# Last stage of a streaming encoder step: the order of the frame products and the expert rows on TensorE

## The chip, the cores and the metric

The kernel runs on one core of a Trainium2 chip. The metric is device time in microseconds (us) for one execution of the whole step, from inputs in device memory to outputs in device memory. The profile calls the engines PE (TensorE), DVE (VectorE), ACT (ScalarE), POOL (GpSimd) and SP (SyncE, which here only issues DMAs); SPq and POOLq are what the profile lists of their instruction queues.

## The reference, cut to what matters

The step is one encoder layer over 2048 prompt frames and 32 sample frames: a projection, two kinds of attention, an output mixer with a LayerNorm, a mixture of experts, and a last LayerNorm. Only the last line concerns us. Each frame has chosen two experts, with two gates, and the layer ends in

```python
x = layer_norm(ALPHA * x + grouped_moe(x, ...), ln2_g, ln2_b)   # ALPHA = 2 ** 0.25
# grouped_moe: for each frame, gate0 * expert0(x) + gate1 * expert1(x)
```

So for a frame with row `h` and the two expert rows `y0` and `y1`, the output is `LN(ALPHA*h + g0*y0 + g1*y1) * ln2_g + ln2_b` over 1024 columns in float32.

## The kernel before, in words

The kernel is written engine by engine, in stages; every engine's instructions stand in the order in which the code issues them, and semaphores tie the engines together. The change is in the last stage, `combine` (from L2971). By then the frames lie in device memory (`scratch_h`), and all expert rows, not yet gated, in `scratch_ypad`.

The stage works on 17 tiles of 128 frames (the last has 32), in four slots: tile `t` uses slot `t % 4` of every buffer, and each slot has its own pair of PSUM banks, `Z[s]`, so that all eight banks are used.

- **SP** loads the frames of tile `t` into `z_h` (L3013; from tile 4 on it first waits until tile `t-4` is summed) and stores finished tiles (L3020). Its order is: loads 0 and 1, the two weight rows, loads 2 and 3, then for each `t`: load `t+4`, store `t`. A store waits for POOL's and DVE's last work on its tile, and load `t+5` stands behind store `t`.
- **POOL** gathers the two expert rows of each frame with two indirect DMAs per tile (L3045), four tiles ahead, and adds the bias to the second half of the columns (L3057).
- **ACT** makes two diagonal matrices of gates per tile, `z_diag` (L3088), takes the square root for the norm (L3106), and applies the norm from PSUM into `z_z` (L3096).
- **PE** sums a tile by matmuls: `ALPHA` times the identity (`z_scaled`) by the frames, which I call the frame product (L3070), and for each of the two experts the diagonal matrix by the gathered rows, the expert rows (L3075). A tile has two halves of 512 columns, so it takes two frame matmuls and four expert matmuls. The frame matmul begins an accumulation, and waits for the frame's load and, from tile 4 on, for the norm of tile `t-4`, which reads the same banks last. The expert matmuls wait for gates and gathered rows. After the last matmul of a tile the semaphore step `sum` is given.
- **DVE** waits for `sum`, takes the statistics from PSUM (L3130 to L3133), multiplies tile `t-1` by the gain and adds half of its bias (L3123, L3124), and then ends tile `t`'s reciprocal and shift (L3137, L3138), for which ACT's norm of tile `t` waits.

Of the kernel before, what the change touches and what calls it, by code (L numbers as in the profile page):

```python
# [19 lines left out]
TILES = NT + 1  # L20
# [2950 lines left out]
def combine(nc, io, keep):  # L2971

    with ExitStack() as ctx:  # L2973
        def sb(name, shape, dt=F32):
            return ctx.enter_context(nc.sbuf_tensor(name, shape, dt))

        def sem(name):
            return ctx.enter_context(nc.semaphore(name))

        SLOTS = 4
# [5 lines left out]
        diag = sb("z_diag", [P, SLOTS, 2, P])  # L2987
# [5 lines left out]
        y_loaded = [sem(f"z_y_loaded{s}") for s in range(SLOTS)]  # L2993
# [3 lines left out]
        diags = Steps(sem("z_diag_steps"), ["diag"])  # L2997
# [4 lines left out]
        HALF = D // 2  # L3002

        def turn(t):
            return t % SLOTS, t // SLOTS

        @block.sync
        def _(sp):
            def load(t):
                s, _ = turn(t)  # L3010
                if t >= SLOTS:
                    sp.wait_ge(*pe.after("sum", t - SLOTS))
                sp.dma_start(h[:, s, :], io["h"][t * P:(t + 1) * P, :]).then_inc(h_loaded[s], 16)  # L3013

            def store(t):
                s, _ = turn(t)
                sp.wait_ge(*pool.after("out", t))
                sp.wait_ge(*done.after("out", t))
                dst = io["y_sample"][0] if t == NT else io["y_prompt"][0, t * P:(t + 1) * P, :]
                sp.dma_start(dst, z[0:NEW if t == NT else P, s, :]).then_inc(stored[s], 16)  # L3020

            load(0)
            load(1)
            sp.dma_start(gain[:, :], io["ln2_g"].broadcast_to([P, D])).then_inc(weights_loaded, 16)
            sp.dma_start(offset[:, :], io["ln2_b"].broadcast_to([P, D])).then_inc(weights_loaded, 16)
            load(2)
            load(3)
            for t in range(TILES):
                if t + SLOTS < TILES:
                    load(t + SLOTS)  # L3030
                store(t)
            for s in range(SLOTS):
                sp.wait_ge(stored[s], 16 * len(range(s, TILES, SLOTS)))
# [25 lines left out]
        @block.tensor  # L3059
        def _(eng):  # L3060
            pe.begin(eng)
            eng.wait_ge(scaled_made, 1)
            for t in range(TILES):
                s, n = turn(t)
                eng.wait_ge(h_loaded[s], 16 * (n + 1))
                if t >= SLOTS:
                    eng.wait_ge(*act.after("norm", t - SLOTS))
                for half in (0, 1):
                    at = slice(half * HALF, (half + 1) * HALF)
                    eng.matmul(Z[s][:, at], scaled[:, :], h[:, s, at], start=True, stop=False)  # L3070
                    if half == 0:
                        eng.wait_ge(*diags.after("diag", t))
                        eng.wait_ge(y_loaded[s], 32 * (n + 1))
                    for i in (0, 1):
                        mm = eng.matmul(Z[s][:, at], diag[:, s, i, :], y[:, s, i, at], start=False, stop=(i == 1))  # L3075
                mm.then_inc(*pe.done("sum"))

        @block.scalar
        def _(eng):
# [63 lines left out]
def build(nc, io):  # L3143

    with ExitStack() as ctx:
# [9 lines left out]
        with ExitStack() as inner:  # L3155
# [28 lines left out]
            mix(nc, io, keep)  # L3184
            experts(nc, io, keep)
        combine(nc, io, keep)

# [37 lines left out]
```

## Time and profile before

| what | value |
|---|---|
| time before, median of 3 runs | 3857.66 us (3852.83 to 3857.68) |
| the profiled execution's own time | 3855.51 us |
| its span, first to last instruction | 3853.7 us |
| first instruction of the last stage (a DMA issue) | 3740.1 us after the span's start |
| first matmul of the stage, first expert row | 3743.80 us, 3753.20 us |
| first and last statistics on DVE | 3759.28 us, 3841.61 us |
| PE busy over the whole span | 3629.9 us (94%) |
| mean granted TensorE clock over the span | 0.97 |

The last stage is the last 113 us or so of the span. All times of day below are us after the span's start. In the rows of the timeline a bracket at the end says how long the engine had been idle, and what released it. The float32 matmuls of this stage show as two records each, so a matmul of the program is "x2" in a row; a matmul's record lasts longer than the distance to the next, as they are pipelined, and the chain of waits gives the distance.

### The profile page before, as it was taken

The numbers are of one execution on the slowest core, as the hardware profiler recorded it, in microseconds if no ns is written. First come the engines' busy times: TensorE is split into PE (matmuls) and PEld (weight loads), VectorE is DVE, ScalarE is ACT, GpSimd is POOL, SyncE is SP. The second block draws the span as 40 slices with busy tenths as digits, with TensorE's granted clock in tenths as the row PEclk, the third lists the DMA queues.
The fourth block names the chain that finished last, engine by engine and source line by source line (L and its number), as shares of the span: only waits on it lengthen the run. The fifth ranks groups of instructions, "written<-read, shape, count | busy, mean of one in ns | idle before, by whom it ended". The sixth has DMA issues, their size and how long they took to land. (4 is left out here: it accounts for less than half of the span.)

```text
span 3853.7 us, 77787 instructions
## 1 busy us (share of the span) xinstructions
PE 3629.9 (94%) x30285; PEld 2174.0 (56%) x30286; DVE 1628.0 (42%) x3569; ACT 954.7 (25%) x1730; POOL 236.8 (6%) x350
## 2 busy tenths in 40 slices
PE   7999997999999999988999989978999999999988
PEld 4444446888888888874555655543333333333333
DVE  1221224666666666666777645560111111111108
ACT  2222221323232323225555521110000000000003
POOL 0000001000000000001111000000000000000005
PEclk9999998999999999988999999988999999999999
DMA  5122212000000000002211152226566567744427
GB/s 218 61 74 74 74 59 61 10 10 19 10 19 10 19 11 19 11 9 81 59 56 56 45 189 92 99 83 269 216 265 255 198 267 283 299 152 159 158 113 305
DMA packets 145519, 430.34 MB, mean 112 GB/s; under 512 B 30696, under 2 KB 73840, under 8 KB 132976
## 3 DMA queue, kind: packets, MB, share of 16 engines
q1 hardware_dynamic: 126736, 359.27, 25.1%
q0 software_dynamic: 11616, 42.21, 3.1%
q10 hardware_dynamic: 6912, 25.17, 1.7%
q8 instruction: 195, 3.19, 0.3%
q14 instruction: 60, 0.49, 0.0%
HBM read 750.99 MB, written 78.27 MB: 215 GB/s over the span
## 5 line engine op out<-in xcount | busy, mean ns | idle before, releaser
L297 PE MATMUL fp<-f_w,f_xT 128*128 128x512 f32 (+1 forms) x1360 | 533.8, 547 | 9.8 <-DMA f_w<-in_w_in 9.5
L716 PE MATMUL rp_pa<-r_xT,w_rwkv 128*128 128x128 f32 x3808 | 483.7, 281 | 11.4 <-DMA r_xT<-scratch_xT 11.4
L716 PEld LDWEIGHTS rp_pa<-r_xT,w_rwkv 128*128 128x128 f32 x3808 | 449.8, 193 | 46.4 <-issue 35.2
L297 PEld LDWEIGHTS fp<-f_w,f_xT 128*128 128x128 f32 x1360 | 244.7, 200 | 262.7 <-issue 261.0
L2851 PE MATMUL e_H<-rows_in,e_xT 128*64 128x512 f32 x768 | 346.0, 604 | 19.7 <-DMA rows_in<-in_moe_w 18.0
L2852 PE MATMUL e_H<-fy,e_xT 128*64 x768 | 345.8, 604 | 0.0
L2870 PE MATMUL e_Y<-e_w,e_gT 128*64 128x512 f32 x768 | 339.8, 595 | 1.0 <-DMA e_w<-in_moe_w 1.0
L2852 PE MATMUL e_H<-e_w,e_xT 128*64 x768 | 339.8, 595 | 0.0
L2851 PE MATMUL e_H<-shared,e_xT 128*64 128x512 f32 x768 | 339.8, 595 | 0.0
L2871 PE MATMUL e_Y<-e_w,e_gT 128*64 x768 | 339.8, 595 | 0.0
L2851 PEld LDWEIGHTS e_H<-rows_in,e_xT 128*64 128x64 f32 x768 | 106.7, 140 | 238.7 <-issue 214.1
L2870 PEld LDWEIGHTS e_Y<-e_w,e_gT 128*64 128x64 f32 x768 | 101.3, 137 | 197.2 <-issue 189.6
L2851 PEld LDWEIGHTS e_H<-shared,e_xT 128*64 128x64 f32 x768 | 101.3, 137 | 197.0 <-issue 191.3
L2948 DVE COPY e_gT<-e_GT 128x512 f32<-128x512 f32 x48 | 33.2, 691 | 346.7 <-PE e_GT L2859 346.7
L1740 ACT ACTIVATE a_z<-a_z,a_low 128x1024 f32<-128x1024 f32 (+4 forms) x192 | 171.1, 895 | 7.1 <-DVE a_inv L1797 4.2
L1306 DVE COPY_PREDICATED r_XT<-r_mask,rp_cb 128x512 f32<-128x512 int32 (+1 forms) x85 | 57.2, 673 | 269.5 <-PE rp_cb L847 263.9
L2960 DVE TENSOR_TENSOR e_g<-e_a,e_H 128x512 f32<-128x512 f32 x48 | 33.0, 687 | 311.5 <-PE e_H L2852 311.5
L2953 DVE COPY e_y<-e_Y 128x512 f32<-128x512 f32 x48 | 33.2, 691 | 307.1 <-PE e_Y L2871 307.1
L1679 PE MATMUL a_turned<-ident,a_z 128*128 128x128 f32 x1088 | 150.6, 280 | 1.8 <-ACT a_pT L1723 1.8
L1693 PE MATMUL a_oT<-a_pT,a_v 128*64 128x256 f32 (+1 forms) x1152 | 149.5, 381 | 2.5 <-issue 2.5
L2921 ACT ACTIVATE e_a<-e_H 128x512 f32<-128x512 f32 x48 | 28.7, 597 | 485.4 <-PE e_H L2852 485.4
L1679 PEld LDWEIGHTS a_turned<-ident,a_z 128*128 128x128 f32 x1088 | 118.4, 141 | 40.8 <-issue 24.8
(434 smaller groups left out, 5601.5 us busy)
## 6 DMA issues: line engine op xcount, KB each, us to landing
e_w<-in_moe_w SPq DMA_DIRECT2D x144, 2048.0 KB
fy<-in_moe_w SPq DMA_DIRECT2D x48, 2048.0 KB
rows_in<-in_moe_w SPq DMA_DIRECT2D x48, 2048.0 KB
shared<-in_moe_w SPq DMA_DIRECT2D x48, 2048.0 KB
scratch_ypad<-e_y ACTq DMA_DIRECT2D x48, 512.0 KB, 2.9
scratch_xT<-f_xT SPq DMA_DIRECT2D x17, 512.0 KB
r_xT<-scratch_xT SPq DMA_DIRECT2D x17, 512.0 KB, 3.7
scratch_h<-m_h SPq DMA_DIRECT2D x17, 512.0 KB, 2.6
```

Source lines behind the costliest of these rows:

```text
L297: mm = eng.matmul(out, xT[:, slot, k, :], w[:, k, a:a + n], start=(k == 0), stop=(k == KD - 1))
L716: mm = eng.matmul(pre_bank(bank)[:, f * P:(f + 1) * P], w[:, d, (i + f) * P:(i + f + 1) * P], xT[:, slot, d, :], start=(d == 0), stop=(d = ...
L1306: eng.copy_predicated(XT[:, :, :, lo:C], each(mask[:, 1, n - 1, lo:C], lo), eight(CB)[:, :, :, lo:C])\
L1679: mm = eng.transpose(turned[n % 3][:, (2 * e + tt) * P:(2 * e + tt + 1) * P], cols(b, tt, e, i * P, P), ident)
L1693: mm = eng.matmul(oT[rows, first:2 * P], v[:, i, rows], pT[:, r, e * 2 * P + first:(e + 1) * 2 * P], start=(i == 0), stop=(i == 2 * b + 1))
L1740: eng.activation(cols(b, tt, e, a, m), cols(b, tt, e, a, m), ACT.Exp, bias=lowest, scale=-1.0, accum_out=total[:, s, h, 2 * tt + e:2 * tt ...
L2851: eng.matmul(out[lower, :], xT[:, s, k, lower], second_of[w][:, k, :], start=on, stop=off)
L2852: mm = eng.matmul(out[upper, :], xT[:, s, k, upper], first_of[w][:, bass.ds(place, 1), k, :], start=on, stop=off)
L2870: eng.matmul(Y[half][lower, :], gT[:, k, lower], second_of["w2"][:, k, at], start=on, stop=off)
L2871: mm = eng.matmul(Y[half][upper, :], gT[:, k, upper], first_of["w2"][:, bass.ds(place, 1), k, at], start=on, stop=off)
L2948: eng.tensor_copy(gT[:, :, :], GT[:, :].rearrange("p (k t) -> p k t", k=KE)).then_inc(*ydve.done("gT"))
L2953: eng.tensor_copy(y[:, s, 512:D], Y[1][:, :]).then_inc(*ydve.done("y1"))
```

## The change

PE's order is changed, and nothing else. Before, a tile's half is frame matmul, two expert matmuls; then the second half in the same way; then the next tile. After, the frame products of tiles 0 to 3, one for each slot, come first. Then come the expert rows of tile `t`, both halves, and behind them the frame product of tile `t+2`, as long as `t+2` is 4 or more and less than 17. The waits stand in front of the same products as before.

```diff
-            for t in range(TILES):
+
+            def frame(t):
                 s, n = turn(t)
                 eng.wait_ge(h_loaded[s], 16 * (n + 1))
                 if t >= SLOTS:
...
                     eng.matmul(Z[s][:, at], scaled[:, :], h[:, s, at], start=True, stop=False)
-                    if half == 0:
-                        eng.wait_ge(*diags.after("diag", t))
-                        eng.wait_ge(y_loaded[s], 32 * (n + 1))
+
+            def experts_rows(t):
+                s, n = turn(t)
+                eng.wait_ge(*diags.after("diag", t))
+                eng.wait_ge(y_loaded[s], 32 * (n + 1))
+                for half in (0, 1):
+                    at = slice(half * HALF, (half + 1) * HALF)
                     for i in (0, 1):
                         mm = eng.matmul(Z[s][:, at], diag[:, s, i, :], y[:, s, i, at], start=False, stop=(i == 1))
                 mm.then_inc(*pe.done("sum"))
+            for t in range(SLOTS):
+                frame(t)
+            for t in range(TILES):
+                experts_rows(t)
+                if SLOTS <= t + 2 < TILES:
+                    frame(t + 2)
```

The start of the stage on PE, before: the rows of tiles 0 and 1. The digit behind `z_Z` is the slot, and L3070 is a frame matmul, L3075 an expert matmul.

```order
L3070 MATMUL z_Z0<-z_h,z_scaled 128x512
L3075 MATMUL z_Z0<-z_y,z_diag 128x512 x2
L3070 MATMUL z_Z0<-z_h,z_scaled 128x512
L3075 MATMUL z_Z0<-z_y,z_diag 128x512 x2
L3070 MATMUL z_Z1<-z_h,z_scaled 128x512
```

The same place after; a frame matmul is now L3071 and an expert matmul L3080. The rows go from the frame products of tiles 0 to 3 up to the expert rows of tile 4.

```order
L3071 MATMUL z_Z0<-z_h,z_scaled 128x512 x2
L3071 MATMUL z_Z1<-z_h,z_scaled 128x512 x2
L3071 MATMUL z_Z2<-z_h,z_scaled 128x512 x2
L3071 MATMUL z_Z3<-z_h,z_scaled 128x512 x2
L3080 MATMUL z_Z0<-z_y,z_diag 128x512 x4
L3080 MATMUL z_Z1<-z_y,z_diag 128x512 x4
L3080 MATMUL z_Z2<-z_y,z_diag 128x512 x4
L3071 MATMUL z_Z0<-z_h,z_scaled 128x512 x2
L3080 MATMUL z_Z3<-z_y,z_diag 128x512 x4
L3071 MATMUL z_Z1<-z_h,z_scaled 128x512 x2
L3080 MATMUL z_Z0<-z_y,z_diag 128x512 x4
```

All four first frame products have moved ahead of the first expert row, and from tile 4 on a frame product stands one whole set of expert rows earlier: slot 0's second frame product (tile 4) now comes before slot 3's first expert rows (tile 3).

The end of the stage on PE, after: the rows of tiles 13 to 16 (slots 1, 2, 3 and 0). Before, the last two tiles each still had their two frame matmuls among their expert matmuls, as in the first fence.

```order
L3080 MATMUL z_Z1<-z_y,z_diag 128x512 x4
L3071 MATMUL z_Z3<-z_h,z_scaled 128x512 x2
L3080 MATMUL z_Z2<-z_y,z_diag 128x512 x4
L3071 MATMUL z_Z0<-z_h,z_scaled 128x512 x2
L3080 MATMUL z_Z3<-z_y,z_diag 128x512 x4
L3080 MATMUL z_Z0<-z_y,z_diag 128x512 x4
```

The last frame product (tile 16) now stands ahead of tile 15's expert rows, and the last two tiles' expert rows follow each other. The other engines' orders are the same as before.

## Rows read from the trace of the kernel before

**Rows 1.** The page's head.
```profile
span 3853.7 us, 77787 instructions
```

**Rows 2.** The chain of waits over the last stage: start, us, what.
```profile
3742.27 10.79 DMA z_y<-scratch_ypad,row
3753.20 3.40 PE z_Z L3075 x4
3756.59 0.86 PE z_Z L3070 x2
...
3841.61 1.31 DVE z_stats L3130 x2
```

**Rows 3.** The timeline where the stage begins: start, us, engine, line, op, idle before.
```profile
3743.80 2.04 PE L3070 MATMUL z_Z<-z_h,z_scaled 128*128 128x512 f32 x2 [7.64 <-DMA z_h<-scratch_h]
...
3759.28 1.29 DVE L3130 BATCH_NORM_STATS2 z_stats<-z_Z 128x6 f32<-128x512 f32 x2 [18.68 <-PE z_Z L3075]
```

**Rows 4.** The timeline of one tile (the seventh) in the middle of the stage.
```profile
3790.11 1.29 DVE L3130 BATCH_NORM_STATS2 z_stats<-z_Z 128x6 f32<-128x512 f32 x2 [0.43 <-PE z_Z L3075]
...
3794.84 0.34 SPq L3020 DMA_DIRECT2D out_y_prompt<-z_z  x1
3794.87 1.20 ACT L3096 ACTIVATE z_z<-z_Z,z_mv 128x1024 f32<-128x1024 f32 x1 [2.79 <-DVE z_mv L3138]
...
3795.22 0.43 SPq L3013 DMA_DIRECT2D z_h<-scratch_h  x1
3795.26 1.29 DVE L3130 BATCH_NORM_STATS2 z_stats<-z_Z 128x6 f32<-128x512 f32 x2 [0.43 <-PE z_Z L3075]
```

**Rows 5.** L3013, frame loads 0 and 1 together, then 2, then 3.
```profile
DMA to landing us min/median/max: 3.5/4.1/4.6
...
L3013 SPq DMA_DIRECT2D z_h<-scratch_h x1: 471/471/471, 3741.9 to 3741.9; - x1
...
DMA to landing us min/median/max: 10.8/10.8/10.8
...
L3013 SPq DMA_DIRECT2D z_h<-scratch_h x1: 525/525/525, 3742.5 to 3742.5; - x1
...
DMA to landing us min/median/max: 12.8/12.8/12.8
```

**Rows 6.** L3013, frame loads 5, 6, 7, 8 one by one; then 9 to 16.
```profile
DMA to landing us min/median/max: 4.5/4.5/4.5
...
DMA to landing us min/median/max: 7.0/7.0/7.0
...
DMA to landing us min/median/max: 6.6/6.6/6.6
...
DMA to landing us min/median/max: 6.0/6.0/6.0
...
DMA to landing us min/median/max: 7.5/8.7/9.0
```

**Rows 7.** L3045, the 26 gathers of tiles 4 to 16.
```profile
DMA to landing us min/median/max: 5.1/7.5/9.7
```

**Rows 8.** Stretches: busy us per engine (count), then granted PE clock, DMA share, GB/s.
```profile
3756.00:3757.00 1.00, 1.00 (x4) 0.52 (x3) 0.00 (x0) 0.00 (x0) 0.00 (x0) 0.94 1.01 410
...
3772.00:3776.00 4.00, 4.00 (x11) 1.78 (x10) 3.47 (x7) 1.74 (x3) 3.09 (x3) 1.00 0.98 352
...
3806.00:3811.00 5.00, 5.00 (x13) 2.29 (x13) 4.44 (x9) 1.84 (x5) 3.61 (x4) 1.00 1.01 406
```

**Rows 9.** A DMA wait of PE in the expert stage: timeline, then a stretch.
```profile
3364.19 1.11 PE L2851 MATMUL e_H<-rows_in,e_xT 128*64 128x512 f32 x1 [4.99 <-DMA rows_in<-in_moe_w]
...
3364.00:3365.00 1.00, 0.81 (x2) 0.39 (x4) 0.00 (x0) 0.00 (x0) 0.00 (x0) 0.50 1.14 479
```

**Rows 10.** PE's waits at L780 (us, times, longest), and a stretch of that stage.
```profile
PE rp_pa L780 <- DVE r_ar L1250: 22.1, 13, 1.7
...
800.00:1400.00 600.00, 574.81 (x10004) 522.02 (x10005) 406.79 (x668) 196.75 (x343) 26.09 (x28) 1.00 0.05 14
```

## The prediction, made before the changed kernel ran

> **What bounds the kernel now.** I read the page first: one core, a span of 3853.7 us [rows 1], of which the changed stage is the last 113 us. Then I followed the chain of waits through that stage [rows 2]. It enters by the gather of tile 0's second expert rows, which lands at 3742.27 + 10.79 = 3753.06. From 3753.20 to 3841.6 it stays on PE without a gap, and then goes to DVE's statistics of the last tile. So PE bounds the stage from the first expert row to the last. Two records, one matmul, take 0.86 us [rows 2]; a tile's six take 5.15 us, which is the distance from 3790.11 to 3795.26 between two tiles' statistics [rows 4]. Check: 101 of the 102 matmuls follow the gather's landing, 101 x 0.858 = 86.7 us, and 3753.20 to 3841.61 is 88.4. The other 1.7 us are the half-speed start: the first expert matmuls take 3.40 us for four records instead of twice 0.86 [rows 2], and the clock is back at full level (0.94) in the slice from 3756 [rows 8].
>
> Next I asked who is second. DVE waits only 0.43 us for PE per tile [rows 4], so its own work is 5.15 - 0.43 = 4.72 us a tile. And the DMA engines are busy 1.01 of the time at 406 GB/s [rows 8]. The stage has three things near their limit, and the change touches the first alone. What it gains on PE must pass the other two.
>
> **The start of the stage.** PE now makes four frame products before it looks at an expert row. Frame 0 is there at 3743.80 [rows 3], frame 1 a little later (4.6 us to landing [rows 5]), so two products run inside the wait that exists today. Even at half speed, four matmuls take 4 x 1.72 = 6.9 us and end at 3750.7: hidden by the gather. Loads 2 and 3 stand behind the two weight rows and land late, at 3741.9 + 10.8 = 3752.7 and at 3742.5 + 12.8 = 3755.3 [rows 5]. The second is 2.2 us after tile 0's expert rows, which now queue behind it. So products 2 and 3 are not hidden. They start at 3752.8 instead of the expert rows at 3753.20.
>
> At which clock? PE has been idle for 2 us or more by then. After a DMA wait of 4.99 us elsewhere the clock was at 0.50 [rows 9]; across 13 waits of at most 1.7 us it stayed at 1.00 [rows 10]. My gap lies between. I take the half-speed start, as before; the other answer is worth 1.0 us less time. Then product 2 ends at 3756.2, product 3 at 3757.9, and tile 0's expert rows (3.43 us) at 3761.3, 2.1 us later than today (3759.28 [rows 3]). Tiles 1 and 2 now need 3.43 us each and end at 3764.8 and 3768.2.
>
> **PE alone.** Up to the end of tile 15 there are 15 frame products (30 matmuls) and 16 sets of expert rows (64): 94 x 0.858 = 80.7, plus the 1.7 of the cold start, from 3752.8: 3835.2. The last set takes only 3.43 us, but DVE needs its 4.72 before it can take the last statistics, so these start at 3839.9 instead of 3841.61. What follows them is unchanged. **Without a new stall the change gains 1.7 us.**
>
> **The new stall.** The frame product of tile t+4 used to stand behind the sum of tile t+3. It now stands behind that of tile t+2: one tile less of time for its load. The load can't go out sooner. On SP it stands behind store t-1, and that waits for DVE and POOL to finish tile t-1, which DVE does after the statistics of tile t. In the rows the statistics start at 3790.11, the store goes at 3794.84 and the load at 3795.22: 5.1 us after [rows 4]. With L for the time to landing, a frame is there 5.1 + L after the statistics. PE wanted it behind the sum of tile t+3, 3 x 5.15 = 15.45 us after that of tile t, so L could be up to 10.3; and the longest was 9.0 [rows 6], which is why nothing shows today. Now it wants it behind the sum of tile t+2, after 2 x 5.15 = 10.3 us: **L must be 5.2 or less.** Only load 5 was (4.5); loads 6, 7 and 8 took 7.0, 6.6 and 6.0, loads 9 to 16 took 7.5 to 9.0 [rows 6].
>
> While PE waits there, the expert rows of tile t+3 wait behind it on PE, and DVE, ACT, both load queues and the stores wait for their sum. So the stall isn't made up; it is spread over three tiles, since a late sum also makes a later load. Tile by tile (load = statistics + 5.1; product = later of landing and the sum two tiles back; next sum 5.15 after; DVE no faster than 4.72):
> - tile 5: load at 3769.9, lands 3774.4, wanted 3773.3: stall 1.1.
> - tile 6: 3774.6, lands 3781.6, wanted 3779.6: stall 2.1.
> - tiles 7 and 8: in time, because these two stalls pushed the want back.
> - tiles 9, 12 and 15: each L - 5.2; the tiles between are in time.
>
> For L from tile 9 on I don't take 7.5 to 9.0. Those came while four transfers of 0.52 MB passed every 5.15 us, at 406 GB/s. With stalls the tile takes about 5.6 us, 376 GB/s, between the 352 of the slice in which loads went quicker and the 406 [rows 8]. I take the mean of loads 6, 7 and 8, 6.5. The three stalls are 1.3 each. Sum: 1.1 + 2.1 + 3 x 1.3 = 7.0 us of stalls, less 1.7: **5.3 us slower.** The bounds are the rows' ends: at L = 4.5 for all, one stall of 1.1 remains and the sum is 0.7 us faster (1.7 with the warmer clock); at 8.8 for all, 16.1 us of stalls, 14.4 us slower.
>
> The Trainium skill, "DMA: Bandwidth & Descriptors", section "Queues, rings and completion order", says each DMA engine serves the queues that have work in turn, a packet at a time. Load 5, with the engines free, landed in 4.5 and so ahead of that; the later ones agree better.
>
> **What costs nothing.** The frame product also waits for the norm of tile t. That begins 4.76 us after the statistics and takes 1.20 [rows 4], 6.0 against 10.3: free. The expert rows of a tile are wanted one frame product (1.72) later than the sum before them, about where they were wanted; gathers took up to 9.7 [rows 7] and were in time. The number of matmuls and weight loads is the same.
>
> **Rivals.**
> A. The loads land early enough (L near 5). For: load 5's 4.5, and stalls unload the DMA engines. Against: any cadence near 5.15 loads them fully. Time: 0.7 to 2.7 us faster; with L = 5.5 from tile 9, 2.3 slower. All of it within 0.2%.
> B. The loads stay as slow as today's loads 9 to 16. For: the cadence changes by under a tenth and the bytes don't. Then tiles 9, 12 and 15 stall 3.6 us each at L = 8.8, and the sum is 3.2 + 10.8 - 1.7 = 12.2 us slower. Stalls of that size also lie above the 1.7 us that left the clock alone, towards the 4.99 that halved it [rows 9, 10]; three half-speed starts more are 3 x 1.7 = 5.2, so up to 17 slower. It is slower by more than 0.2% (7.7 us) from L = 7.3 on. The Trainium skill, "TensorE: Matmul & The Clock Gate", section "HAM oscillation", describes this pattern: waits for DMA between short bursts, each of which begins cold; the trace agrees for the long wait, and no row shows one of 3 us.
> C. The stage keeps its time since PE is bound by work and the reordering removes none. For: the count of matmuls is equal. Against: three matmuls do move into the first wait. It would give the median, 3857.7, to within a microsecond.
>
> **The numbers.** The profiled execution took 3855.51 us, 2.1 below the median of the three runs. 3855.51 + 5.3 = 3860.8 for an execution like it, and against the median 3857.66 + 5.3 = 3863.0, which I predict. A measurement of this kernel can tell about 0.2%, 7.7 us, from no change. Chances: the forecast, 1 to 7.7 slower, 0.57; A 0.10; C 0.05; B 0.25; something that gains over 7.7 us, for which I see no mechanism, 0.03. Faster 0.03, within 0.2% 0.72, slower 0.25. The range goes from 3855 (A, with the runs' own spread) to 3872 (most of B).
>
> **What would show it.** In the new profile: two frame products well before 3753 and two from about 3752.8; first statistics near 3761 (without the cold clock near 3760); PE waiting at L3071 for z_h, for a microsecond or two, at about every third tile from tile 5, 4 to 10 us in all; landings of 5.5 to 7; statistics of the last tile about 4.7 us after those before; DVE's wait for PE no longer an even 0.43. I am wrong if L3071 shows no waits in the middle (A), if they exceed 3 us or the clock falls inside the stage (B), or if tile 0's sum comes sooner than today.

## The result, and the profile after

The changed kernel takes 3870.33 us (median of 7 runs, 3862.27 to 3871.73), the kernel before 3857.68 us beside it (7 runs, 3850.24 to 3859.1). The ratio is 1.0034, with a 95% interval of 1.0024 to 1.0044: slower by about 13 us, in the direction of the forecast (5.3 us) and two and a half times its size, close to what rival B gave (12.2).

The profiled execution has a span of 3868.7 us, 15.0 more than before [rows 1]. Of these, 3.5 lie ahead of the stage, in work that the change doesn't touch: its first load goes out at 3743.63 instead of 3740.12. From here on I therefore read the stage by itself, from that issue to the start of the last tile's statistics: 101.5 us before (3841.61 [rows 2]), and 3856.57 - 3743.63 = 112.9 us after. The stage is 11.4 us longer.

PE's waits in that stage, after (us in all, times, longest):

```profile
PE z_Z L3071 <- DMA z_h<-scratch_h: 20.6, 8, 7.5
```

And one by one, in PE's timeline (start, us, what, idle before):

```profile
3747.19 6.46 PE L3071 MATMUL z_Z<-z_h,z_scaled 128*128 128x512 f32 x8 [7.53 <-DMA z_h<-scratch_h]
3757.95 6.22 PE L3071 MATMUL z_Z<-z_h,z_scaled 128*128 128x512 f32 x8 [4.30 <-DMA z_h<-scratch_h]
...
3781.04 1.98 PE L3071 MATMUL z_Z<-z_h,z_scaled 128*128 128x512 f32 x4 [1.42 <-DMA z_h<-scratch_h]
...
3786.82 1.98 PE L3071 MATMUL z_Z<-z_h,z_scaled 128*128 128x512 f32 x4 [0.37 <-DMA z_h<-scratch_h]
...
3794.35 1.98 PE L3071 MATMUL z_Z<-z_h,z_scaled 128*128 128x512 f32 x4 [2.11 <-DMA z_h<-scratch_h]
...
3812.00 1.98 PE L3071 MATMUL z_Z<-z_h,z_scaled 128*128 128x512 f32 x4 [1.87 <-DMA z_h<-scratch_h]
...
3819.38 1.98 PE L3071 MATMUL z_Z<-z_h,z_scaled 128*128 128x512 f32 x4 [1.96 <-DMA z_h<-scratch_h]
...
3841.32 1.98 PE L3071 MATMUL z_Z<-z_h,z_scaled 128*128 128x512 f32 x4 [1.02 <-DMA z_h<-scratch_h]
```

Where [rows 3] showed one wait for a frame, at the very start, there are eight. The first (7.53) is the old one. The second (4.30) is the new wait of the start, for frame 2. The other six are the new stall, ahead of tiles 5, 6, 7, 10, 11 and 15: 8.75 us in all.

The chain of waits names the load of frame 2 (the first row) and the loads behind three of the six (start, us, what):

```profile
3745.44 12.46 DMA z_h<-scratch_h
...
3757.95 6.22 PE z_Z L3071 x8
3764.16 3.45 PE z_Z L3080 x8
...
3785.45 8.85 DMA z_h<-scratch_h
...
3794.35 1.98 PE z_Z L3071 x4
3796.33 3.43 PE z_Z L3080 x8
3799.76 1.72 PE z_Z L3071 x4
...
3810.07 9.27 DMA z_h<-scratch_h
...
3835.15 6.12 DMA z_h<-scratch_h
```

In [rows 2] the chain entered PE once and stayed there; now it leaves PE for a frame load and comes back. Two sizes can be read here, with the ends of matmuls as the profile models them. A frame product takes 1.72 us where PE goes on without a break and 1.98 where it had waited. And frames 2 and 3 together take 6.22 us, 2.8 more than their four matmuls at full speed: they begin at half clock, as this stretch shows (columns as in [rows 8]).

```profile
3757.00:3759.00 2.00, 1.05 (x2) 0.54 (x3) 0.00 (x0) 0.00 (x0) 0.00 (x0) 0.50 1.04 424
```

DVE's timeline has the first statistics and the last two:

```profile
3767.71 1.29 DVE L3143 BATCH_NORM_STATS2 z_stats<-z_Z 128x6 f32<-128x512 f32 x2 [23.61 <-PE z_Z L3080]
...
3851.93 1.29 DVE L3143 BATCH_NORM_STATS2 z_stats<-z_Z 128x6 f32<-128x512 f32 x2 [0.43 <-PE z_Z L3080]
...
3856.57 1.28 DVE L3143 BATCH_NORM_STATS2 z_stats<-z_Z 128x6 f32<-128x512 f32 x2
```

The first statistics come 24.1 us after the first load issue (before: 3759.28 - 3740.12 = 19.2 [rows 3]). The last two are 4.64 us apart, and the last has no wait for PE: DVE's own pace sets the end.

### The profile page after: what moved, and what is told of

It reads as the page before. It is cut to its first block and busy times, and to the rows that moved or that the text cites. A ratio compares the mean times of both kernels' runs of the same rounds, so it can differ in the third digit from the quotient of the medians.

```text
span 3868.7 us, 77787 instructions
## 1 busy us (share of the span) xinstructions
PE 3640.9 (94%) x30285; PEld 2182.0 (56%) x30286; DVE 1628.1 (42%) x3569; ACT 954.5 (25%) x1730; POOL 236.7 (6%) x350
## 3 DMA queue, kind: packets, MB, share of 16 engines
q1 hardware_dynamic: 126736, 359.27, 25.1%
## 5 line engine op out<-in xcount | busy, mean ns | idle before, releaser
L297 PE MATMUL fp<-f_w,f_xT 128*128 128x512 f32 (+1 forms) x1360 | 533.5, 547 | 10.8 <-DMA f_w<-in_w_in 10.4
L2870 PEld LDWEIGHTS e_Y<-e_w,e_gT 128*64 128x64 f32 x768 | 101.3, 137 | 197.2 <-issue 189.6
L2851 PEld LDWEIGHTS e_H<-shared,e_xT 128*64 128x64 f32 x768 | 101.3, 137 | 197.0 <-issue 191.3
```

Of the source, the lines that this page charges most:

```text
L297: mm = eng.matmul(out, xT[:, slot, k, :], w[:, k, a:a + n], start=(k == 0), stop=(k == KD - 1))
L2851: eng.matmul(out[lower, :], xT[:, s, k, lower], second_of[w][:, k, :], start=on, stop=off)
L2870: eng.matmul(Y[half][lower, :], gT[:, k, lower], second_of["w2"][:, k, at], start=on, stop=off)
```

## The experiments

The theory: a frame product that stands one tile earlier wants its load sooner than SP, behind the last store, can send it. The rivals: the loss is the late and half-clocked start; or the DMA engines are full, and asking earlier only moves the wait; or two sets of expert rows in a row make DVE the bound. All stage times are from one profile each, first load issue to last statistics; "mid waits" are PE's waits for `z_h` after the start.

| kernel | first statistics, us | mid waits, us | stage, us | time against before (95%) |
|---|---|---|---|---|
| before | 19.2 | 0 | 101.5 | 1 |
| changed | 24.1 | 8.8 | 112.9 | 1.0034 (1.0024 to 1.0044) |
| changed, loads ahead of stores | 22.4 | 0 | 100.8 | 0.9999 (0.9990 to 1.0008) |
| two frames first, two tiles ahead | 18.0 | 6.7 | 109.6 | 1.0017 (1.0008 to 1.0026) |
| four frames first, one tile ahead | 22.4 | 0.7 | 102.2 | 0.9995 (0.9985 to 1.0005) |
| before, loads ahead of stores | 19.0 | 0 | 101.3 | 0.9999 (0.9990 to 1.0009) |
| changed, small stores | 21.6 | 6.3 | 109.8 | 1.0019 (1.0006 to 1.0031) |
| changed, three tiles ahead | 22.7 | 27.1 | 144.9 | 1.0127 (1.0112 to 1.0142) |
| two frames first, loads ahead of stores | 20.2 | 0 | 102.0 | 1.0001 (0.9993 to 1.0010) |
| changed, one gather per tile | 22.0 | 3.2 | 104.1 | 1.0007 (0.9996 to 1.0017) |
| changed, filler matmuls at the start | 21.3 | 6.2 | 108.2 | 1.0050 (1.0033 to 1.0067) |
| two frames first, loads ahead, late weights | 15.1 | 0 | 97.0 | 0.9984 (0.9975 to 0.9993) |
| before, late weights | 18.0 | 0 | 100.4 | 0.9986 (0.9977 to 0.9995) |

**The loads sent sooner, in the changed kernel.**

```diff
                 if t + SLOTS < TILES:
                     load(t + SLOTS)
-                store(t)
+                if t:
+                    store(t - 1)
+            store(NT)
```

> The changed kernel, but SP issues the frame load of tile t+4 ahead of the store of tile t-1 instead of behind it. I read the stage from its first load issue to the start of the last statistics: 101.5 us before, 112.9 after. Theory (the loads go out too late for a frame product that stands one tile earlier): the load goes out some 5 us sooner, so the waits for z_h from tile 5 on (8.8 us in all) vanish; stage 102 to 104 us, time 9 to 10 us under the changed kernel and within 3 us of before. Rival (the DMA engines are full, so that an earlier request only waits longer): landings grow from 6 to 9 us to 11 to 14, the waits stay, stage 110 to 113.

PE's only waits for frames are the two of the start (PE's waits, columns as above):

```profile
PE z_Z L3073 <- DMA z_h<-scratch_h: 12.2, 2, 7.5
```

And the load of tile 6 goes out with the statistics of tile 2. First DVE's timeline there, then SP's:

```profile
3771.94 1.28 DVE L3145 BATCH_NORM_STATS2 z_stats<-z_Z 128x6 f32<-128x512 f32 x2
```
```profile
3772.42 0.42 SPq L3013 DMA_DIRECT2D z_h<-scratch_h  x1
```

The load follows the statistics by 0.5 us; in [rows 4] it was 5.1. The whole loss is gone, so the load's issue was its cause. The stage came out shorter than the 102 to 104 us that I expected: of the 12.1 us between it and the changed kernel, 1.7 are an earlier first sum. Full DMA engines were not the cause. A stretch of 30 us (columns as in [rows 8]):

```profile
3795.00:3825.00 30.00, 30.00 (x71) 13.29 (x70) 26.67 (x46) 11.92 (x24) 21.85 (x18) 1.00 1.03 416
```

In the changed kernel the same stretch had a DMA share of 0.95 and 353 GB/s, and PE was busy for 26.17 us of it. So the DMA engines are fuller here, and yet PE is busy without a break. The loads do land later, as the rival had it, but by little: those of tiles 8 to 16 in 8.6 to 9.5 us, as far as the trace kept their completion events. Two tiles less 0.5 us allow 9.8, so not much room is left.

**The start as before, the middle as in the change.**

```diff
-            for t in range(SLOTS):
+            for t in range(2):
                 frame(t)
             for t in range(TILES):
                 experts_rows(t)
-                if SLOTS <= t + 2 < TILES:
+                if 2 <= t + 2 < TILES:
                     frame(t + 2)
```

> The changed kernel, but only frames 0 and 1 are made first; the frame product of tile t+2 follows the expert rows of tile t from t = 0 on. So loads 2 and 3 no longer stand ahead of tile 0's expert rows, and the rest is as in the changed kernel. Theory: the waits for z_h in the middle stay (7 to 10 us), only the start gets 3 to 5 us shorter; stage 107 to 110 us, time 5 to 9 us over before. Rival (the loss is the start: the late loads 2 and 3 and the half clock there): the loss goes, stage 101 to 103.

PE's waits for frames in it:

```profile
PE z_Z L3071 <- DMA z_h<-scratch_h: 14.4, 6, 7.7
```

All but the first of its six waits lie in the middle: 6.7 us. The stage is 8.1 us longer than before, against 11.4 in the changed kernel. Some 1.7 of the 8.1 are a stretch at half clock (shown in the last section): from the product at 3810.51 to the next statistics it took 7.15 us, against 5.45 behind the changed kernel's wait of 2.11. The changed kernel's middle has no such stretch. So the middle is the larger part of the loss, some 6 to 8 us of the 11.4, and the start, with loads 2 and 3 ahead of tile 0's expert rows, is the rest.

**The start as in the change, the middle as before.**

```diff
-                if SLOTS <= t + 2 < TILES:
-                    frame(t + 2)
+                if SLOTS <= t + 1 < TILES:
+                    frame(t + 1)
```

> The changed kernel's start (four frame products first), but from tile 4 on the frame product of tile t+1, not t+2, follows the expert rows of tile t, as late as in the kernel before. Theory: no wait for z_h after the start; the start stays 4 to 5 us late to the first sum, which the matmuls already made give back; stage 101 to 104 us, time within 3 us of before. Rival (start and clock): stage stays at 108 to 113. Rival (expert rows back to back make DVE the bound): DVE has no wait for PE from tile 5 on and the stage stays over 108.

PE's waits, for frames and for gathered rows:

```profile
PE z_Z L3071 <- DMA z_h<-scratch_h: 12.8, 3, 7.6
PE z_Z L3080 <- DMA z_y<-scratch_ypad,row: 1.1, 2, 0.6
```

One wait of 0.7 us is left in the middle, and two of the gathers' that the profile of before did not have. The late start (22.4) is given back by the products already made. DVE does set the pace at first, 4.63 to 4.65 us a tile without a wait for PE from tile 2 to tile 6, but then 5.15 returns and the stage is not over 108: that the expert rows stand back to back is not what the changed kernel loses.

**The kernel before with the loads sent sooner.** The edit is that of the first experiment, in the old order of PE.

> The kernel before with SP's order of the first experiment alone (load t+4 ahead of store t-1). Theory: nothing waited for a frame there after tile 0, so nothing changes: stage 101 to 102 us, time within 2 us of before; landings a little shorter or equal. Rival (the order of loads and stores by itself moves the gathers or the engines' load): stage 2 us or more away from 101.5.

Nothing changed: 101.3 us, and a ratio of 0.9999. What the first experiment gave is thus the load's issue as the new order needs it, and not a better order of transfers in itself.

**One more tile ahead.**

```diff
-                if SLOTS <= t + 2 < TILES:
-                    frame(t + 2)
+                if SLOTS <= t + 3 < TILES:
+                    frame(t + 3)
```

> The changed kernel with the frame product of tile t+3 behind the expert rows of tile t, one more tile ahead (four at first, as in the changed kernel). Theory (a frame product placed k tiles ahead gives its load (4-k) tiles less the 5.1 us to its issue): now 5.15 us after the statistics, against 5.1 + L, so PE waits L or nearly so at every second tile, 2T = 5.1 + L + 5.15; with L of 5 to 7 the tile takes 7.6 to 8.6 us, 12 tiles lose 30 to 42 us; stage 135 to 150 us, time 25 to 40 us over the changed kernel. Rival (the waits come from full DMA engines, which are less loaded here): L falls to 4.5 or less and the loss is under 20 us over the changed kernel.

One of its waits in PE's timeline, and the stretch in which it lies:

```profile
3792.10 3.78 PE L3071 MATMUL z_Z<-z_h,z_scaled 128*128 128x512 f32 x4 [4.53 <-DMA z_h<-scratch_h]
```
```profile
3792.00:3794.00 2.00, 1.90 (x3) 0.87 (x4) 0.33 (x1) 1.63 (x3) 1.54 (x3) 0.50 1.00 395
```

The stage is 144.9 us, 32.0 more than in the changed kernel. Five of its waits are 4.2 to 4.6 us, at every second tile, and after them the clock is at half level and the product takes up to 3.78 us. The loads that follow a pause landed in 4.3 to 4.7 us, those that follow the burst before by some 5 us in 5.1 to 7.1. The rule of tiles ahead held: PE waits nearly the whole landing at every second tile. The time came out by 0.93% of 3858, 36 us, over the changed kernel, as expected, but partly by luck. The loads that PE waits for landed quicker than the 5 to 7 us of my sum, as the rival had it, and the half clock, which my sum left out, made up for that: from the product at 3792.10 to the next statistics it took 7.65 us, against 5.45 in the changed kernel.

**What makes the landing long? First the stores, cut to an eighth of their columns.**

```diff
-                sp.dma_start(dst, z[0:NEW if t == NT else P, s, :]).then_inc(stored[s], 16)
+                sp.dma_start(dst[:, 0:D // 8], z[0:NEW if t == NT else P, s, 0:D // 8]).then_inc(stored[s], 16)
```

> The changed kernel with each store of the last stage cut to 128 of its 1024 columns; the other columns of y_prompt and y_sample are not written. Every engine's order and waits are as in the changed kernel; only 0.46 of 2.1 MB per tile no longer moves. Theory (a frame load lands late because it goes out in one burst with a store ahead of it and two gathers beside it): landings of tiles 6 to 15 fall from 6 to 9 us to 4.5 to 6, PE's waits for z_h after the start fall from 8.8 us to under 3, stage from 112.9 to 105 to 108 us. Rival (the landing is a fixed delay of the load, whatever else moves): landings and waits as in the changed kernel, stage 111 to 114.

The median landing (issues, KB each, median us to landing) is that of the changed kernel, 6.7. In both profiles it rests on 8 of the 17 loads, those whose landing the profile gives. Below it are PE's waits for frames:

```profile
z_h<-scratch_h SPq DMA_DIRECT2D x17, 512.0 KB, 6.7
```
```profile
PE z_Z L3071 <- DMA z_h<-scratch_h: 16.6, 8, 7.6
```

My theory of the burst failed as I had put it: the bytes of the store ahead in the same queue are not the main thing that delays a load. Of the 16.6 us, 10.3 are the two waits of the start, so the mid waits fell only from 8.8 to 6.3. The stage is 3.1 us shorter, and 2.5 of that is its earlier first sum. Two things limit this reading. The cut stores still stand ahead of the loads and move in as many packets as before (126736 on their queue over the whole execution, in both profiles); stores of fewer packets were not tried. And behind a wait of 2.46 us the clock fell to half level for a while, which lengthens this stage and not the changed kernel's.

**Then one gather of the two left out.**

```diff
-                for i in (0, 1):
+                for i in (0,):
                     eng.indirect_dma_start(out=y[0:rows, s, i, :], ...
...
-                eng.wait_ge(y_loaded[s], 32 * (n + 1))
+                eng.wait_ge(y_loaded[s], 16 * (n + 1))
...
-                        mm = eng.matmul(Z[s][:, at], diag[:, s, i, :], y[:, s, i, at], ...
+                        mm = eng.matmul(Z[s][:, at], diag[:, s, i, :], y[:, s, 0, at], ...
```

> The changed kernel with one gather per tile instead of two: the second expert's rows are left out, and both expert products read the first expert's rows, so the outputs are not the layer's. Orders and waits are else the same; 0.52 of 2.1 MB per tile no longer moves. Cutting the stores by about as much left the landings at a median of 6.7 us. Theory (a frame load that follows the burst before it by only 5 us lands late because the gathers of that burst are still moving): landings of tiles 6 to 15 fall to 4 to 5.5 us, PE's waits for z_h after the start from 8.8 to under 3 us. Rival (the landing in a run of loads 5 us apart is 6 to 9 us whatever else moves): landings and waits as in the changed kernel.

The median landing (here of all 17 loads), PE's timeline at its two mid waits, and the landings of loads 9 to 16:

```profile
z_h<-scratch_h SPq DMA_DIRECT2D x17, 512.0 KB, 4.5
```
```profile
3778.50 1.98 PE L3071 MATMUL z_Z<-z_h,z_scaled 128*128 128x512 f32 x4 [1.40 <-DMA z_h<-scratch_h]
...
3785.69 1.98 PE L3071 MATMUL z_Z<-z_h,z_scaled 128*128 128x512 f32 x4 [1.77 <-DMA z_h<-scratch_h]
```
```profile
DMA to landing us min/median/max: 4.2/4.4/4.6
```

Two waits are left, ahead of tiles 5 and 6. Tile 5's load took 4.5 us. Those of tiles 6 and 7, sent only 4.3 and 4.6 us behind the load before, still took 7.3 and 6.6 with one gather. From tile 9 on the loads landed in 4.2 to 4.6 us, at the same 5.15 us a tile at which loads 9 to 16 of the kernel before took 7.5 to 9.0 [rows 6], and PE never waited again. So one gather less does shorten a frame load's landing, where nearly the same number of bytes left out of the stores had done little. That points to the gathers beside it and those of the tile before. It does not show that gathers count as such: with this edit the number of packets fell too, and with the small stores it did not.

**The clock at the start.** Four filler matmuls in the wait for frame 2.

```diff
             for t in range(SLOTS):
+                if t == 2:
+                    for _ in (0, 1):
+                        for half in (0, 1):
+                            at = slice(half * HALF, (half + 1) * HALF)
+                            eng.matmul(Z[3][:, at], scaled[:, :], h[:, 1, at], start=True, stop=True)
                 frame(t)
```

> The changed kernel with four filler matmuls (frame 1 into slot 3's banks, begun anew by frame 3's own product later) in PE's wait for frame 2's load. Theory of the start (products 2 and 3 run at half speed because PE idled for 4.3 us): PE idles under 1.5 us, the clock is at full level when frame 2 lands, products 2 and 3 take 3.4 us of PE instead of 6.2 (the second may wait for its load); the first statistics come 1 to 2 us sooner after the first load issue (24.1 us in the changed kernel; 22.4 in two other profiles). Rival (the start is set by load 3 alone, or the clock falls all the same): first statistics at 22.4 to 24.5.

Frames 2 and 3 in PE's timeline, and the stretch around the first:

```profile
3753.85 1.98 PE L3071 MATMUL z_Z<-z_h,z_scaled 128*128 128x512 f32 x4 [1.10 <-DMA z_h<-scratch_h]
...
3756.41 1.98 PE L3071 MATMUL z_Z<-z_h,z_scaled 128*128 128x512 f32 x4 [0.58 <-DMA z_h<-scratch_h]
```
```profile
3753.00:3755.00 2.00, 1.15 (x3) 0.68 (x4) 0.00 (x0) 0.00 (x0) 0.00 (x0) 1.00 1.03 420
```

The clock stayed full, each product took 1.98 us, and the first statistics came at 21.3 us, 2.8 sooner than in the changed kernel. Not all of that is the clock. Load 3 landed 15.8 us after the first load issue (2.5 + 13.3) instead of 16.8 (2.3 + 14.5), and here its product waited for it. At full clock the changed kernel's would have waited too, so the half clock cost it some 1.7 us, an estimate from these rows. And the timed runs are no faster than the changed kernel's (1.0050, 1.0033 to 1.0067). The profiled execution took 3862.82 us, the least of its four, whose median is 3874.72; where the others lose the time its profile can't tell, and that stays open. What a full clock at the start gives is shown in one profile; in time it is not shown.

**Two frames first, and the loads ahead of the stores**, the second and the first experiment together.

> The second and the first experiment together: frames 0 and 1 first, frame product of tile t+2 behind the expert rows of tile t, and SP's load t+4 ahead of store t-1. Theory: neither the late loads 2 and 3 nor the middle waits are left; PE has 98 matmuls (84.1 us) behind the first gather's landing and a cold start of 1.7, DVE's 4.6 us a tile ends it; stage 100 to 101 us, time 0 to 3 us under before, which a comparison of five rounds can hardly tell from none. Rival (two frames ahead costs something besides the load's wait): stage over 102.

No wait for a frame after the first, and DVE waits an even 0.42 or 0.43 us for PE, as before. Its stage, 102.0 us, missed my 100 to 101: its first expert rows ran at half clock for longer (first statistics at 20.2). In time it equals the kernel before. Being early on PE is worth nothing measurable there.

**A version meant to beat both: the weights of the last norm loaded late.** To the last version this adds

```diff
-            sp.dma_start(gain[:, :], io["ln2_g"].broadcast_to([P, D])).then_inc(weights_loaded, 16)
-            sp.dma_start(offset[:, :], io["ln2_b"].broadcast_to([P, D])).then_inc(weights_loaded, 16)
             load(2)
             load(3)
+            sp.wait_ge(y_loaded[1], 32)
+            sp.dma_start(gain[:, :], io["ln2_g"].broadcast_to([P, D])).then_inc(weights_loaded, 16)
+            sp.dma_start(offset[:, :], io["ln2_b"].broadcast_to([P, D])).then_inc(weights_loaded, 16)
```

with DVE's and POOL's waits for these rows moved to their first use.

> A version meant to beat both: frames 0 and 1 first and then two tiles ahead, SP's load t+4 ahead of store t-1, and the two weight rows of the last norm (1 MB) loaded only when tile 1's expert rows have landed, so that the frames and first gathers don't share the DMA engines with them. Theory (the start of the stage is a queue of transfers): the first expert row starts 9 to 10.5 us after the first load issue instead of 13, the middle keeps its 5.15 us a tile; stage 96 to 99 us, time 3 to 5 us under before. Rival (the gathers' landing is their own issue and not the queue): first expert row stays at 12.5 to 13, stage 100 to 101.

The first expert rows on PE, and the last statistics on DVE:

```profile
3754.88 3.67 PE L3084 MATMUL z_Z<-z_y,z_diag 128*128 128x512 f32 x8 [2.33 <-DMA z_y<-scratch_ypad,row]
...
3840.48 1.28 DVE L3148 BATCH_NORM_STATS2 z_stats<-z_Z 128x6 f32<-128x512 f32 x2
```

The first load goes out at 3743.46, so the first expert row starts 11.4 us later, not 9 to 10.5, and the stage is 97.0. The time is 0.9984 of before, some 6 us under.

**The late weights alone, in the kernel before.**

> The kernel before with the late weight rows alone, PE's and SP's other order as before. Theory: the same gain at the start, without the 1.2 us that the two frame products in the first wait give; stage 97 to 100 us, time 2 to 4 us under before. If it equals the version with the new order, the frame products ahead are worth nothing by themselves.

0.9986 (0.9977 to 0.9995), the same within the interval, though its stage in the one profile is 100.4 us, a little over the 97 to 100 expected. The late weights beat both kernels, by little: 0.14 to 0.16% under the kernel before, with intervals that leave out 1. The new order on top adds nothing that these runs can tell.

## Why the prediction was right, and where its size was off

The direction, the new wait, its place and its cause were forecast. That the time fell into the range (3870 of 3855 to 3872) owes something to the range's width: the slowdown of 13 us lies past the 1 to 7.7 us that had a chance of 0.57, in the part above 7.7 us that had 0.25. The sum missed in three terms, all in the same direction.

- **PE bounds the stage; the new wait is the frame load.** Right. It stands at L3071, between a sum and the frame product two tiles on, and sending the load sooner removes it.
- **Without a new stall 1.7 us are gained.** Not refuted: the stage was 0.7 shorter without mid waits (loads ahead of stores) and 0.7 longer with 0.7 us of them (one tile ahead), at starts of 22.4 us, where 21.2 was forecast.
- **The start.** Forecast: frame 2 at 12.7 us after the first issue, a cold start worth 1.7. Measured in the changed kernel: 14.3, because load 2 took 12.46 us and not 10.8 [rows 5], and products that took 2.8 us longer than at full clock, since the half clock reached both. Together 2.7 us more than forecast, the largest of the three. Four other profiles with the same start had the first statistics at 21.6 to 22.7 against 24.1 here and 21.2 forecast, so this term varies by some 2 us from one execution to the next.
- **The step whose reasoning failed is the landing.** "With stalls the tile takes about 5.6 us, 376 GB/s ... I take the mean of loads 6, 7 and 8, 6.5." The landings didn't follow the mean rate. A stall makes one burst late, but the tiles between still follow at 4.6 to 5.2 us, with the gathers before them moving. The loads behind the six waits took 4.5, 6.0, 8.85, 7.0, 9.27 and 6.1 us. By the trace's completion events those of tiles 7 to 16 took 4.3 to 9.3, 7.1 in the mean, so the mean was little off; the spread was what the forecast lacked. It had stalls of 1.1, 2.1 and 0 for tiles 5, 6 and 7 and 3.9 from tile 9 on; measured were 1.42, 0.37 and 2.11, and 4.85 (1.87 + 1.96 + 1.02). Tile 7 is the clearest miss: DVE, at 4.64 us a tile, let its load go out only 4.6 us behind the one before, and it took 8.85. All stalls: 8.75 instead of 7.0 (its own terms add up to 7.1). Rival B's 8.8 at every tile was too long, and its half clock didn't come; its sum was near for other reasons.
- **A term that I left out.** Each wait also cost 0.26 us in the product behind it (1.98 against 1.72): six times, 1.6 us.
- The sum by these measurements: 5.3 forecast, + 2.7 for the start, + 1.8 for the stalls (8.75 against 7.0), + 1.6 = 11.4 us, which is what the stage grew by. The timed ratio, 13 us (9 to 17), holds it.
- **The clock in the middle.** No fall there in the changed kernel's profile. My sum gave stalls of up to 2.1 us no cost in clock; that held here, but not in other kernels, as the last section shows.
- **What speaks of shared queues.** The Trainium skill, "DMA: Bandwidth & Descriptors", section "Queues, rings and completion order", has the engines serve the queues in turn. The runs agree so far as a load next to one gather instead of two landed in 4.2 to 4.6 us instead of 7.5 to 9.0 at the same 5.15 us a tile. They don't bear out that part of my estimate in which the bytes of the store ahead, in the load's own queue, delay the load by their own time: an eighth of them left the median at 6.7.

## What to carry to other kernels

Before a product is moved ahead in an in-order queue, ask when its operand's transfer can be sent, not only whether it is in time today: slack that the trace doesn't show (here 10.3 us allowed and up to 9.0 used) is used up first, and then the wait holds up all work behind it. Move the transfer's issue along with its use; here that was a change of three lines in the program of the queue that sends it. And take a landing time from rows with the same neighbours at the same distance, not from a mean rate.

## What the runs showed of the hardware

- Nearly equal amounts of bytes left out do not do the same. With one gather less, 0.52 MB a tile, frame loads at 5.15 us a tile landed in 4.2 to 4.6 us, where the kernel before had 7.5 to 9.0. With the stores cut by 0.46 MB a tile, in as many packets, the median landing stayed at 6.7 us.
- A frame product behind a DMA wait took 1.98 us instead of 1.72 at full clock, as the chain of waits counts it, in every one of the changed kernel's six mid waits.
- The clock's answer to a short wait varied. In the changed kernel it stayed full after 2.11 us; with two frames first it was at 0.50 soon after a wait of 1.95:

```profile
3810.51 2.79 PE L3071 MATMUL z_Z<-z_h,z_scaled 128*128 128x512 f32 x4 [1.95 <-DMA z_h<-scratch_h]
```
```profile
3812.00:3814.00 2.00, 2.00 (x4) 0.73 (x3) 1.29 (x3) 0.64 (x1) 1.84 (x2) 0.50 0.98 383
```
